# Reordering one core's three-layer network: pair turns in one go, a start in halves, window keys by pieces, banks of their own for the branch chunks

## What is computed

```python
# layer 0: MLA (8 heads) beside stick-breaking attention (8 heads), then SwiGLU
# layer 1: chunked band attention (16 heads), then SwiGLU, then rms_norm
# last layer, four attention groups of 8 heads in branches A, B (three dilations), C (window 128):
proj = rms_norm(h) @ w_in_2                    # q, k, v of each group, gates
o_g  = softmax(q_g k_g^T / 8 + bias_g) v_g     # 8 heads of 64, 256 tokens
br_i = (combined o of branch i * swish gate) @ w_branch[i]
out  = h + (sum_i sigmoid(gate_i) * br_i) @ w_out_2
```

## Time and profile before

| What | Value |
|---|---|
| median of three runs | 1002.76 us |
| lowest and highest of them | 1002.12 and 1002.85 us |
| the profiled execution's own time | 1001.44 us |
| its span | 999.7 us |
| instructions in it | 13330 |

### The profile page before, as it was taken

The page is one execution under the profiler, slowest core; times in us unless marked ns, Lnnn a source line. Parts: engine busy times, 40 slices in busy tenths (PEclk is TensorE's granted clock), DMA queues, the critical chain, the costliest instruction groups (busy, mean ns, idle before and its releaser), DMA issues.

```text
span 999.7 us, 13330 instructions
## 1 busy us (share of the span) xinstructions
PE 983.8 (98%) x4920; PEld 791.9 (79%) x4920; DVE 629.3 (63%) x782; ACT 594.9 (60%) x929; POOL 12.2 (1%) x22
## 2 busy tenths in 40 slices
PE   7999999999999999999999999999999998999998
PEld 5888788888888777788888888877777776778877
DVE  5676775555556765675555557866757657776654
ACT  5777665454546655465454445776767576866571
POOL 1000000000000000000000000000000000000000
PEclk9999999999999999999999999999999999999999
DMA  8536265755563633556756663644344234336551
GB/s 275 172 115 210 77 199 200 240 174 204 170 208 127 210 127 127 168 175 226 252 192 228 210 206 131 210 168 169 126 135 157 86 127 156 111 112 213 205 173 43
DMA packets 106041, 170.26 MB, mean 170 GB/s; under 512 B 3988, under 2 KB 65302, under 8 KB 106000
## 3 DMA queue, kind: packets, MB, share of 16 engines
q1 hardware_dynamic: 103360, 161.23, 47.6%
q0 software_dynamic: 2304, 8.37, 2.6%
q10 hardware_dynamic: 336, 0.10, 0.0%
HBM read 168.58 MB, written 1.11 MB: 170 GB/s over the span
## 4 chain that ended last, share of the span: by engine, by line
PE 96%; ACT 2%; DVE 2%; issue 0%; DMA 0%; ACTq 0%; DVEq 0%
PE acc L434 14%; PE acc L436 13%; PE acc L435 13%; PE acc L485 12%; PE pair_ps L436 7%; PE pair_ps L434 7%; PE pair_ps L435 7%; PE acc L713 3%; PE acc L536 3%; PE turn_ps L609 2%; PE acc L630 2%; PE pair_ps L597 2%; PE acc L577 1%; PE pair_ps L596 1%; PE turn_ps L503 1%; PE turn_ps L434 1%
## 5 line engine op out<-in xcount | busy, mean ns | idle before, releaser
L1665 DVE TENSOR_TENSOR w_lo<-w_raw,w_hi 128x2048 fp32r<-128x2048 f32 (+2 forms) x155 | 345.5, 2232 | 127.4 <-ACT w_hi L1026 127.1
L1026 ACT ACTIVATE w_hi<-w_raw 128x2048 fp32r<-128x2048 f32 (+2 forms) x155 | 288.3, 1863 | 80.6 <-PE acc L436 35.5
L434 PE MATMUL acc<-w_hi,uT_hi 128*128 128x512 f32 (+3 forms) x552 | 221.3, 401 | 3.2 <-DVE w_lo L2096 2.6
L436 PE MATMUL acc<-w_hi,uT_lo 128*128 128x512 f32 (+3 forms) x552 | 212.8, 385 | 0.0
L435 PE MATMUL acc<-w_lo,uT_hi 128*128 128x512 f32 (+3 forms) x552 | 211.9, 384 | 0.0
L434 PEld LDWEIGHTS acc<-w_hi,uT_hi 128*128 128x128 f32 x552 | 104.1, 189 | 30.7 <-issue 9.2
L434 PE MATMUL pair_ps<-w_hi,uT_hi 128*128 128x512 f32 x320 | 126.5, 395 | 0.0
L436 PE MATMUL pair_ps<-w_hi,uT_lo 128*128 128x512 f32 x320 | 124.8, 390 | 0.0
L435 PE MATMUL pair_ps<-w_lo,uT_hi 128*128 128x512 f32 x320 | 124.6, 390 | 0.0
L436 PEld LDWEIGHTS acc<-w_hi,uT_lo 128*128 128x128 f32 x552 | 103.9, 188 | 21.2
L435 PEld LDWEIGHTS acc<-w_lo,uT_hi 128*128 128x128 f32 x552 | 104.4, 189 | 17.5
(11 more groups left out here) (230 smaller groups left out, 1233.4 us busy)
## 6 DMA issues: line engine op xcount, KB each, us to landing
w_raw<-in_w_in SPq DMA_DIRECT2D x46, 1024.0 KB
w_raw<-in_w_gate SPq DMA_DIRECT2D x44, 512.0 KB
w_raw<-in_w_up SPq DMA_DIRECT2D x44, 512.0 KB
w_raw<-in_w_down SPq DMA_DIRECT2D x22, 1024.0 KB
w_raw<-in_w_out SPq DMA_DIRECT2D x12, 1024.0 KB
w_raw<-in_w_qkv SPq DMA_DIRECT2D x16, 512.0 KB
w_raw<-in_w_branch SPq DMA_DIRECT2D x6, 1024.0 KB
bias<-rel_rows POOLq DMA_DIRECT2D x5, 1024.0 KB, 7.2
```

Of the source, the lines that this page charges most:

```text
L434: mm(o, xh, wh[:, k, :], start=first and k == 0, stop=False)
L436: done = mm(o, xl, wh[:, k, :], start=False, stop=last and k == len(kts) - 1)
L1026: activation(w_hi[:, slot, 0:width], w_raw[:, slot, 0:width], ACT.Copy).then_inc(hi_done, 1)
L1665: v.tensor_tensor(w_lo[:, slot, 0:width], w_raw[:, slot, 0:width], w_hi[:, slot, 0:width].bitcast(f32), ALU.subtract).then_inc(lo_done, 1)
```

## The change

1. **Turns in one go.** Pairs 1 and 2 are turned into the two `turn_ps` banks, pairs 0 and 3 into `acc[2]`. Pairs 0, 1 and 2 go ahead of block 1 of step 0 and pair 3 behind step 0. ACT copies three pairs at step 0 and one at step 1. `turn_outputs(0)` and `(1)` go behind steps 3 and 4, and `turn_outputs(2)` goes behind `values(3)`.
2. **Shared keys by pieces.** DVE writes the first two key places and releases `qk_ready`, then writes the other six and releases `keys_spread`. In the window group PE turns pair 0 after the first signal, and pairs 1 and 2 behind step 0 after the second. DVE takes `token_outputs(3)` between the key sums and the root.
3. **Kept-busy beginning.** PE runs 8 matmuls of ones by ones (128x128 fp32, no result used) ahead of the turns of the input and 8 behind them. Both first units are loaded, split and multiplied in halves, and the copies of the input alternate with the halves. `distances` goes behind the first half of the second unit and waits for two tables. POOL loads the other four only after the second unit has arrived.
4. **Banks of their own.** All branch chunks but the first use `acc[2:4]`. The waits for copies move back by one chunk. The closing projection starts with block 0, which needs the gate copies alone.
5. **Order of the splits.** The fourth call puts the splits of steps 4 and 5 late, and the fifth call that of step 2. DVE's `token_outputs` goes ahead of a late split. At the first branch step DVE splits one more unit ahead of its multiply.

The core of the diff (declarations, loads and repeated calls left out):

```diff
-        qk_banks = [qkT_ps[:, :]] + acc_banks
+        qk_banks = [qkT_ps[:, :]] + turn_banks + [qkT_ps[:, :]]
+        def branch_banks(i, half):
+            return acc[2:4] if (i, half) != (0, 0) else acc[0:2]
...
-            for dst, src in ((onehot[:, :], bucket_onehot), (dist_m, dist_mask),
-                             (m_strict[:, :], strict_mask),
+            for dst, src in ((onehot[:, :], bucket_onehot), (dist_m, dist_mask)):
+                pool.dma_start(dst, src).then_inc(tables, 16)
+            pool.wait_ge(raw_full[1], 32)
+            for dst, src in ((m_strict[:, :], strict_mask),
...
+            def keep_busy(times):
+                for _ in range(times):
+                    mm(acc[3][:, 0:P], ones[:, 0:P], ones[:, 0:P], start=True, stop=True)
             def turn_input():
+                pe.wait_ge(eps_set, 2)
+                keep_busy(8)
                 pe.wait_ge(ident_full, 16)
...
+                keep_busy(8)
...
                                 group_ready(qk, copied)
                                 pe.wait_ge(out_read, pair0)
-                                turn_pair(kind, 0)
-                            if s == 1:
-                                turn_pair(kind, 1 + blk)
-                            if s >= 3 and blk == 1:
-                                turn_outputs(s - 3, pair0, turn0, outs)
+                                for t in range(1 if n.window else 3):
+                                    turn_tokens(t, qk_banks[t])
                             if s == 5 and blk == 1:
                                 if closing:
                                     closing()
                                 attention_step(kind, 5, pair0, turn0)
+                                turn_outputs(2, pair0, turn0, outs)
                         chunk_unit(...)
+                        if s == 0 and n.window:
+                            pe.wait_ge(keys_spread, 1)
+                            for t in (1, 2):
+                                turn_tokens(t, qk_banks[t])
+                        if s == 0:
+                            pe.wait_ge(qkT_read, turn0 + 1)
+                            turn_tokens(3, qk_banks[3])
                         if s == 1:
-                            turn_pair(kind, 3)
+                            pe.wait_ge(qkT_read, turn0 + 3)
                         if s < 5:
                             attention_step(kind, s, pair0, turn0)
+                        if s in (3, 4):
+                            turn_outputs(s - 3, pair0, turn0, outs)
...
                 none = ()
-                first_unit()
-                halves(uT_hi, uT_lo, range(4, 8), 512, False, True, ((distances,), none))
+                unit_in_halves(0)
+                unit_in_halves(4, distances)
...
-                    if i or half:
-                        chunk(uT_hi, uT_lo, KT, 512)
+                    step = 2 * i + half
+                    if step:
+                        chunk(uT_hi, uT_lo, KT, 512, reads=0 if step == 1 else 1)
+                    if step == 1:
+                        pe.wait_ge(out_read, n.pair)
...
-                    chunk(oT_hi, oT_lo, 4, 512, x_kt=4 * (i % 2))
+                    chunk(oT_hi, oT_lo, 4, 512, x_kt=4 * (i % 2), banks=branch_banks(i, half),
+                          reads=(0, None)[step] if step < 2 else 1)
+            pe.wait_ge(acc_read, n.chunk * 2 - 2)
+            pe.wait_ge(turned_lo, n.bank)
+            proj_half((4, 5), 0, True, False)
             pe.wait_ge(acc_read, n.chunk * 2)
-            pe.wait_ge(turned_lo, n.bank)
-            proj_unit((4, 5), True, False)
+            proj_half((4, 5), 1, True, False)
...
                     attention_step(kind, s, n.pair, head0, bias_of)
+                    if 3 <= s:
+                        token_outputs(s - 3, n.pair, head0)
                     if s in late:
                         slot_step(prefetch[s])
-                    if 3 <= s:
-                        token_outputs(s - 3, n.pair, head0)
...
-            split_banks(uT_hi, uT_lo, 0, 4, stream_banks[MIX0], MIX0)
-            first_unit()
-            split_banks(uT_hi, uT_lo, 4, 4, stream_banks[MIX0][2:], MIX0)
-            split_unit(1)
+            input_pair(0)
+            half_of(0, 0)
+            input_pair(2)
+            half_of(0, 1)
+            input_pair(4)
+            half_of(1, 0)
+            input_pair(6)
+            half_of(1, 1)
...
+                token_outputs(3, n.pair, 24)
                 dve.wait_ge(summed, n.sums)
                 sharpen(*[stat[:, i, 0:4] for i in range(4)], HD)
...
+                spread(0, 0, 2).then_inc(qk_ready, 1)
+                spread(0, 2, 2)
+                spread(1, 0, 4).then_inc(keys_spread, 1)
...
-                               prefetch=(UNIT, UNIT, 1024, 1024, UNIT, UNIT), after_unit={2: head_norm(0)}, late=(4,))
+                               prefetch=(UNIT, UNIT, 1024, 1024, UNIT, UNIT), after_unit={2: head_norm(0)}, late=(4, 5), last=False)
...
-                    if step:
-                        for _ in range(2):
-                            slot_step()
+                    for _ in range((0, 1, 2)[min(step, 2)]):
+                        slot_step()
...
                     if step == 0:
                         last_gate()
+                        slot_step()
```

More of the change, by code:

```diff
@@ L47 @@
 GAIN_ROWS = GAIN_COL[FINAL] + 8
-CONSTS = 6 * 16
+CONSTS = 4 * 16
 LN_EXP_TABLES = 6
@@ L456, in chunk_unit, with unit_in_halves @@
                     n.chunk = n.chunk + 1
-            def first_unit():
+            def unit_in_halves(kt0, between=None):
+                count = kt0 // 4 + 1
                 for k0, ready in ((0, first_lo), (2, lo_done)):
-                    pe.wait_ge(ready, 1)
+                    if between and k0:
+                        between()
+                    pe.wait_ge(ready, count)
                     parts = [w[:, k0:k0 + 2, :] for w in unit_parts(4, 512)]
                     for blk in range(TB):
-                        done = half_unit(acc[blk][:, :], uT_hi, uT_lo, range(k0, k0 + 2), parts, blk, k0 == 0, False)
+                        last = kt0 + k0 == 6
+                        done = half_unit(acc[blk][:, :], uT_hi, uT_lo, range(kt0 + k0, kt0 + k0 + 2), parts, blk,
+                                         kt0 + k0 == 0, last)
+                        if last and blk == 0:
+                            done.then_inc(blk0_done, 1)
                 done.then_inc(unit_used, 1)
@@ L1534, in swiglu, with half_of, input_pair @@
                 n.written, n.bank = n0 + NF, b0 + NF
[L1537 to L1548 removed]
+            def half_of(unit, half):
+                full = raw_full[unit] if half else (first_full, second_full)[unit]
+                c = slice(1024 * half, 1024 * half + 1024)
+                act.wait_ge(full, 32)
+                activation(w_hi[:, unit, c], w_raw[:, unit, c], ACT.Copy).then_inc(hi_done if half else first_hi, 1)
+            def input_pair(kt):
+                split_banks(uT_hi, kt, 2, stream_banks[MIX0][kt // 2:], MIX0)
+            act.wait_ge(gains_full, 32)
+            input_pair(0)
[6 more added lines that the diff above has]
+            half_of(1, 1)
             for blk in range(TB):
@@ L1638, in _ @@
                     slot_step()
-                    copy_chunk(lambda blk: [(branch_out[:, blk, :], acc[blk][:, :], ACT.Copy, 1.0)])
+                    banks = branch_banks(i, half)
+                    copy_chunk(lambda blk: [(branch_out[:, blk, :], banks[blk][:, :], ACT.Copy, 1.0)])
             slot_step()
@@ L1907, in project, with project_and_attend @@
                         done[s]()
-            def project_and_attend(units, kind, head0=0, bias_of=None, done={}, prefetch=(UNIT,) * 6, after_unit={}, late=(), closing={}):
+            def project_and_attend(units, kind, head0=0, bias_of=None, done={}, prefetch=(UNIT,) * 6, after_unit={}, late=(), closing={}, last=True):
                 for s in range(6):
```

100 lines of the change are left out of this document (49 added, 51 removed).

## The result

The changed kernel takes 991.64 us (median of 4 runs, 991.50 to 991.91) against 1002.44 us of the kernel before in the same measurement. The ratio is 0.9893, 95% interval 0.9876 to 0.9910. I had said 995.8 us, range 993.9 to 999.0. The profiled execution took 991.65 us with a span of 989.8 us. Both are 9.8 us less than before.

The account below looks back on a forecast made before the run. TensorE, busy 983.8 of 999.7 us, was taken as the bound, so only its idle or slow time could pay. 2.5 + 0.2 + 3.2 + 1.1 = 7.0 us off the 1002.8 median gave 995.8 us, range 993.9 to 999.0.

Parts of the forecast that it names:

- The start, 2.5: Input and first weight units: third unit starts at 22.23 instead of 24.77, from an earlier first half and the clock.
- their lower bound: Dummies at the start: two records per product at a transpose's price, 0.46 us each, 3.7 for eight at low clock.
- Turns in one go, 0.2: Five attention groups: three fewer breaks of PE's weight stream in each, at 0.00 to 0.05 us per break, give 0.2 us.
- My bound of 0.75 for the 15 breaks: Five groups: three fewer breaks in each, at 0.00 to 0.05 us, give 0 to 0.75 us.
- A loop turn as long as before, within 0.15: Sign that the forecast is right: a loop turn's length stays the same within 0.15 us.
- The late groups, 3.2: Window group and the one before: PE's waits shrink by 1.2, 0.8 (window keys) and 1.2 (two ACT waits), sum 3.2 us.
- the 1.2: PE's wait for `token_outputs(1)`, behind a DVE split of 2.29 us: goes when that order is turned round.
- the 0.7: Window group: PE's wait for exponentials behind a 1.90 us rounding; goes as `late=(2,)` puts the rounding behind them.
- The branches, 1.1: Branches and closing projection: PE's waits of 0.4 us for a DVE split and 0.7 us go, 1.1 us.
- The clock did not fall again: Rival, the start: the clock falls again, 1.5 us return, perhaps 1.8 more; 997.3 to 999.1 us; chance 21%.
- The form in which transposes count as idleness: Clock rival's form, the start: only real matmuls lift the clock, 1.8 + 1.5 us are lost; 999.1 us; chance 4%.
- The small waits did not move: Rival, window group and start: small waits move instead of going, 1.6 + 1 us return; 998.4 us; chance 16%.

Follow-up runs that it names:

- the ten breaks: Changed kernel with the first two outputs' turns back in the middle of steps 3 and 4, 10 more breaks in five groups: 992.41 us.
- the two band versions: Changed kernel with the band group's turns in pairs too: 995.02 us; then with ACT's copies of pairs 6 and 7 ahead of pair 5's exponentials: 991.39 us.

## Why the prediction was right and where it failed

The time is 4.2 us below the 995.8. About 2.9 of it are terms of the sum that were too small (turns 1.6, branches 1.0, late groups 0.3), and the rest, about 1.3, is what the sum was taken off.

*The start, 2.5.* Right, mark by mark, against the profiled execution: 2.50. The clock stayed up, the dummies cost their lower bound, and no split came late. That it fits to 0.04 us is luck: with the same start the third unit begins between 21.92 and 22.68 in six other traces (the start alone, the changed kernel once more, the ten breaks, the late groups' order left out, and the two band versions).

*From what the sum was taken off, 1.0 to 1.3.* This step failed. The profiled execution of before (1001.44) was one of the lower level, and the three runs shown (1002.12 to 1002.85) lie by the upper one. I saw the 1.3 us between them and took 7.0 off the median as if both were the same kernel at work. On the upper level the first 12 or so weight matmuls run at the low clock (0.43 apart), where on the lower one it is 8 behind five fast ones. The start is worth 3.9 there, and the change does away with both. A start with halves and both times eight dummies has shown one level (seven runs of the start alone, eight of the changed kernel), and the upper level has more slow matmuls in both of its traces, which are of kernels with the old start. Why the clock is high at the first weight matmul behind the same 16 transposes in one execution and low in the next, these runs don't show.

*Turns in one go, 0.2.* This step failed in its size, and it is the largest part of the miss: 0.35 in each of five groups, 1.8. The row that I took the earlier trace rows starts at the first transpose, so that it doesn't hold what is lost ahead of it, and I priced a break at 0.00 to 0.05 by it. Measured, a break of four token turns cost 0.04, 0.04, 0.11 and 0.06 in the band group and 0.11 in the loop, and an output's two transposes cost 0.08 in a break of their own. The offsets within one loop turn give 0.11 for the merged token turns, 0.075 and 0.097 for the outputs of steps 3 and 4, and 0.07 for the outputs placed behind the values in step 5. My bound of 0.75 for the 15 breaks did not contain 1.8. "A loop turn as long as before, within 0.15" was wrong as well: it is 0.35 to 0.38 shorter.

*The late groups, 3.2.* 3.5 by the offsets, and the 0.3 that stays for the keys is what was said. The causes were shared out wrongly. I put the 1.2 down to DVE's order and the 0.7 to the late rounding; the turns in one go take both by themselves. (The 0.5 they take as I had said.) That PE comes for the outputs a block later would explain the 1.2; what took the 0.7 there was not followed up. The edits of the order carry 1.9.

*The branches, 1.1.* Right in place, mis-sized: 2.1 by the times and 2.0 by the offsets. I added up idle rows. A wait that interrupts the weight stream costs its row, plus the 0.16 by which the ends of matmuls are drawn into the next one, plus about 0.1 at re-entry; and two waits of 0.16 had no row at all. The same error, smaller, is in the late groups.

In sum, on the profile: 1.6 (turns) + 0.9 to 1.0 (branches) + 0.3 (late groups) = 2.8 to 2.9 on top of 7.0, and 9.8 is what the spans show. With 1.0 for the level of the median the gain of 10.8 is complete.

*The rivals.* The clock did not fall again in either trace of the changed kernel (all starts at 0.22 to 0.24), and its eight runs lie within 0.41 us, which leaves no room for a low stretch like that of before. Without the second eight dummies four runs of five have a lower mean clock (0.996 to 0.998). The form in which transposes count as idleness does not fit three traces without first dummies, in which the clock was up by the first weight matmul (its successor starts 0.33 or 0.34 behind it); two others, in which it was not (0.60 and 0.59), show that 16 transposes are not always enough. The small waits did not move.

## What to carry to other kernels

Ahead of subtracting from a median, look whether the profiled execution belongs to the same level as the runs, and price a wait by the distance between the starts of the instructions around it, not by the idle time in its row. A wait of 2 us in a full TensorE stream can cost nearly twice its length, as the clock may fall behind it (to 0.57 in the one trace that has such a wait): moving copies ahead of a 1.9 us rounding was worth 3.6 us. Cheap filler ahead of and behind the load-bound beginning paid in every run here only together with first units in halves (1.9 us); alone it gave 1.3 us in some runs and almost nothing in others.

## What the runs showed of the hardware that I had not expected

- The clock column reads 1.00 ahead of the first rise that it records, whatever the clock is: over the first dummies (0.24 each, 0.12 later), and where 9 matmuls of 512 columns took 3.00 us (two traces). The distances between starts show the clock.
- With the same dummies from 1.15 us on, the distance between starts fell from 0.21 to 0.11 at times between 4.0 and 6.5 us in the nine traces that have them. So when the clock rises varies by execution.
- Transposes alone had lifted the clock by 8.2 us in one trace: 0.21 us each, and 0.12 per record of the same size right behind them. In two others it was low when the weight stream began at 11.2, behind the same 16 transposes and 2.65 idle us, and 12 matmuls ran slow (0.60 or 0.59, then 0.43 apart). Both are executions of the upper level.
- After idle stretches of 1.9 and 2.6 us at the start and of 2.0 us in the full stream the clock fell (0.52, 0.50 and 0.57 in the windows behind them), and after one of 3.2 us it didn't. The one of 2.0 cost 3.6 us in all.
- A break in the weight stream costs 0.04 to 0.11 us for four transposes that have a break to go to, and 0.08 for two.
